# Seven-product pieces whose weight sums are made partly by accumulating transfers, in a two-block transformer kernel

## What is computed

```python
x = x + jnp.square(jax.nn.relu(h @ w_ff1[i])) @ w_ff2[i]
...
def swiglu(x, w_gate, w_up, w_down):
    return (jax.nn.silu(x @ w_gate) * (x @ w_up)) @ w_down
```

## Time and profile before

| | |
|---|---|
| median of three runs | 1417.21 us |
| the profiled execution, its own time | 1417.31 us |
| its span | 1415.5 us |
| TensorE busy (matmul / weight load) | 1408.9 / 1200.0 us |
| VectorE, ScalarE, GpSimd busy | 1159.3, 809.4, 26.6 us |
| read from HBM | 246.59 MB, 175 GB/s |

### The profile page before, as it was taken

The page is one execution under the profiler, slowest core; times in us unless marked ns, Lnnn a source line. Parts: engine busy times, 40 slices in busy tenths (PEclk is TensorE's granted clock), DMA queues, the critical chain, the costliest instruction groups (busy, mean ns, idle before and its releaser), DMA issues.

```text
span 1415.5 us, 22899 instructions
## 1 busy us (share of the span) xinstructions
PE 1408.9 (100%) x9209; PEld 1200.0 (85%) x9209; DVE 1159.3 (82%) x1601; ACT 809.4 (57%) x1095; POOL 26.6 (2%) x93
## 2 busy tenths in 40 slices
PE   9999999999999999999999999999999999999999
PEld 8988778888888888889878888888888887888887
DVE  6876776898877998988868888888888798688886
ACT  7735474655446655555766555556555557665552
POOL 0000000000001100000000000000000000000000
PEclk9999999999999999999999999999999999999999
DMA  8441335555555555455334554545545453355543
GB/s 336 152 150 62 105 107 207 177 181 208 194 215 179 192 195 195 176 195 197 135 120 174 186 199 181 208 174 195 196 179 202 161 177 146 115 203 188 182 179 116
DMA packets 36105, 249.12 MB, mean 176 GB/s; under 512 B 4128, under 2 KB 4256, under 8 KB 6688
## 3 DMA queue, kind: packets, MB, share of 16 engines
q1 hardware_dynamic: 35712, 247.46, 48.9%
q10 hardware_dynamic: 288, 0.19, 0.1%
HBM read 246.59 MB, written 1.05 MB: 175 GB/s over the span
## 4 chain that ended last, share of the span: by engine, by line
PE 97%; DMA 1%; ACT 1%; DVE 0%; issue 0%; SPq 0%; DVEq 0%; ACTq 0%
PE ps L2192 24%; PE ps L2107 16%; PE ps L2109 15%; PE ps L2108 15%; PE ps L2199 13%; PE ps L2182 2%; PE ps L2367 2%; PE ps L2181 1%; DMA raw<-ws 1%; PE ps L2281 1%; PE ps L2580 1%; PE ps L2560 1%; PE ps L2569 1%; PE ps L2352 0%; PE ps L2178 0%; ACT hi L2623 0%
## 5 line engine op out<-in xcount | busy, mean ns | idle before, releaser
L2991 DVE TENSOR_TENSOR lo<-raw,hi 128x2048 fp32r<-128x2048 f32 (+1 forms) x230 | 525.1, 2283 | 74.0 <-ACT hi L2623 71.3
L2623 ACT CAST hi<-raw 128x2048 fp32r<-128x2048 f32 (+1 forms) x230 | 438.8, 1909 | 195.5 <-PE ps L2109 105.9
L2192 PE MATMUL ps<-h,hi 128*128 128x512 f32 x1504 | 359.2, 390 | 0.0
L2192 PEld LDWEIGHTS ps<-h,hi 128*128 128x128 f32 x1504 | 276.4, 188 | 52.4
L2107 PE MATMUL ps<-hi,a 128*128 128x512 f32 x532 | 210.8, 396 | 0.0
L2109 PE MATMUL ps<-hi,a 128*128 128x512 f32 x532 | 207.6, 390 | 0.0
L2108 PE MATMUL ps<-lo,a 128*128 128x512 f32 x532 | 207.4, 390 | 0.0
L2199 PEld LDWEIGHTS ps<-h,lo 128*128 128x128 f32 x1504 | 192.2, 190 | 7.9
L2199 PE MATMUL ps<-h,lo 128*128 128x256 f32 x1504 | 194.4, 282 | 0.0
L2820 ACT COPY a<-ps 128x256 f32<-128x256 f32 x208 | 75.9, 372 | 152.6 <-PE ps L2192 80.4
L2107 PEld LDWEIGHTS ps<-hi,a 128*128 128x128 f32 x532 | 99.9, 188 | 22.2 <-issue 2.4
(11 more groups left out here) (385 smaller groups left out, 1782.5 us busy)
## 6 DMA issues: line engine op xcount, KB each, us to landing
raw<-ws SPq DMA_DIRECT2D x229, 1024.0 KB, 4.8
X<-xin SPq DMA_DIRECT2D x8, 256.0 KB, 5.5
raw<-ws SPq DMA_DIRECT2D x2, 512.0 KB, 6.5
out<-X SPq DMA_DIRECT2D x4, 256.0 KB, 2.1
small<-small SPq DMA_DIRECT2D x1, 992.5 KB, 12.8
const<-const SPq DMA_DIRECT2D x1, 900.0 KB, 6.6
a<-row SPq DMA_DIRECT2D x1, 512.0 KB, 6.0
const<-const SPq DMA_DIRECT2D x1, 388.0 KB, 14.2
```

What stands on the lines that cost most here:

```text
L2192: t = e.matmul(b2(s["slots"][u]), wh[:, k, 128 * u:128 * u + 128], h2[:, k, :, :], start=k == 0, stop=last)
L2623: e.copy(hi[j % NSPL][:, n], raw[j % NRAW][:, n]).then_inc(hi_ready, 1)
L2991: e.tensor_tensor(lo[j % NSPL][:, n], raw[j % NRAW][:, n], hi[j % NSPL][:, n].bitcast(F), ALU.subtract).then_inc(lo_ready, 1)
```

## The change

Gated down projections take seven products in pieces 1, 3, 4, 5, 6 and 7 of nine. For them there are two sets of `WL`, `WH`, `WS`, used in turn, so that a piece's sums wait for product 4 of the seven-product piece two before it; the second set lies where the normed activations were, free once the last up product is done. `ffn2` keeps its five pieces and its one set.

Signs are turned so that every weight sum is an addition. GpSimd issues three transfers of 256 KB for each piece: block 4 of the piece from HBM into `WS`, then, once `raw` is there, block 1 added onto block 2 inside `raw`, then, once the first has landed, block 2 from HBM added onto `WS`. ScalarE's `hi` waits for the second. VectorE's `w_sums`, now two instructions, waits for the second and the third. In the gated projections every unit but the first has the order 3, 1, 2, 7, 6, 4, 5 (the last unit 1, 2, 6, 7, 5, 4, 3), and waits for the weights' sums at its first product that uses one. `ffn2` and first units have 7, 6, 4, 5, 3, 1, 2 (the last of `ffn2` 1, 6, 7, 5, 4, 3, 2). The recombination keeps eight instructions.

```diff
@@ -28,7 +28,7 @@
-SEVENS = {"a": (1, 3, 5, 7), "s": (3, 5, 7, 9, 11)}
+SEVENS = {"a": (1, 3, 4, 5, 6, 7), "s": (3, 5, 7, 9, 11)}
...
@@ -488,14 +491,24 @@
                 self.H, self.L = acts
-                self.WL, self.WH, self.WS = (sums([128, 3, 512], R), sums([128, 3, 512], R), sums.again([128, 3, 512]))
+                self.sums = [(ar_([128, 3, 512], R), ar_([128, 3, 512], R), ar_.again([128, 3, 512])) for ar_ in sums]
                 self.ML = [mixed([128, 3, 128], R) for _ in range(n)]
...
 
-        by_src = {"a": Sevens(4, (aH, aL), Arena(14 * 4096), Arena(17 * 4096), (sgm[0], sgm[1], sgs[0])),
-                  "s": Sevens(5, (sH, sL), Arena(h_at - arena0), late_ar, (rl[0], rl[1], h_rest))}
+        by_src = {"a": Sevens(6, (aH, aL), [Arena(14 * 4096), Arena(h_at - arena0)], Arena(17 * 4096), (sgm[0], sgm[1], sgs[0])),
+                  "s": Sevens(5, (sH, sL), [Arena(h_at - arena0)], late_ar, (rl[0], rl[1], h_rest))}
+
+        def sums_before(j):
+
+            return sum(n <= j and n % NRAW == j % NRAW for n in sevens)
+
+        def sums_of(j):
+
+            src, unit = sevens[j]
+            return by_src[src].sums[unit % len(by_src[src].sums)]
+
         sevens = {}
...
@@ -596,17 +609,27 @@
 
+        summed = {}
+        high_at = {}
+
+        def sums_early(j):
+
+            if j in sevens and j not in summed:
+                src, unit = sevens[j]
+                sets = len(by_src[src].sums)
+                in_h = unit == sets - 1
+                summed[j] = [wsum_v.add() for _ in range(2)]
+                emit("w_sums", dve=1.4, j=j, nth=sum(n < j for n in sevens), own=summed[j], used=sum(n < j for n in sevens) - min(unit, sets - 1),
+                     after=freed[j - SEVENS[src][unit] - 1] if in_h else None)
+
         def split_hi():
...
             next_split["hi"] += 1
-            sums = None
+            sums_early(j)
+            emit("hi", act=1.9, j=j, after=freed.get(j - NSPL), sums=j in sevens)
             if j in sevens:
-                sums = wsum_v.n + 1
-                emit("w_sums", dve=2.6, j=j, own=[wsum_v.add() for _ in range(3)],
-                     used=sum(n < j for n in sevens), after=freed[j - NSPL] if sevens[j] == ("s", 0) else None)
-            emit("hi", act=1.9, j=j, after=freed.get(j - NSPL), sums=sums)
-            if j in sevens:
-                emit("w_hi", act=1.4, j=j, v=wsum_v.n, v_hi=wsum_a.add())
+                emit("w_hi", act=1.4, j=j, v=summed[j][-1], v_hi=wsum_a.add())
+                high_at[j] = wsum_a.n
             hi_due[j] = cur[0]
...
@@ -615,7 +638,7 @@
-                emit("w_lo", dve=1.7, j=j, v_hi=wsum_a.n, v=wsum_v.add())
+                emit("w_lo", dve=1.7, j=j, v_hi=high_at[j], v=wsum_v.add())
...
@@ -824,15 +847,21 @@
             opens, closes = unit == 0, unit == len(SEVENS[src]) - 1
-            need = {"own": unmet(needs(k + 1, 0)), "mixed": unmet((mix_v.sem, mixed[k])), "sums": unmet((wsum_v.sem, seven_at[i]))}
-            steps = (("7", extra[7]), ("6", extra[6]), ("4", main[1, 0]), ("5", extra[5]), ("3", main[0, 1]), ("1", extra[1]),
-                     ("2", main[0, 0]))
-            if closes:
-                steps = (steps[5], steps[1], steps[0], steps[3], steps[2], steps[4], steps[6])
-            for n, (which, sl) in enumerate(steps):
+            slots = {"1": extra[1], "2": main[0, 0], "3": main[0, 1], "4": main[1, 0], "5": extra[5], "6": extra[6], "7": extra[7]}
+            if src == "a" and unit:
+                order = "1267543" if closes else "3127645"
+            else:
+                order = "1675432" if closes else "7645312"
+            first_sum = min(order.index(which) for which in "674")
+            for n, which in enumerate(order):
+                need = {}
+                if n == 0:
+                    need.update(lo=(lo_ready, i + 1), own=unmet(needs(k + 1, 0)), mixed=unmet((mix_v.sem, mixed[k])))
+                if n == first_sum:
+                    need.update(sums=unmet((wsum_v.sem, seven_at[i])))
                 apart = which in "1567"
-                emit("seven", i=i, which=which, k=k, src=src, unit=unit, slot=sl, opens=apart and opens, closes=apart and closes,
-                     frees=which == "4", uses=which == "2", need=need if n == 0 else {})
+                emit("seven", i=i, which=which, k=k, src=src, unit=unit, slot=slots[which], opens=apart and opens,
+                     closes=apart and closes, frees=which == "4", uses=n == 6, need=need)
                 yield "pe"
...
@@ -2267,7 +2295,7 @@
-                    elif s["uses"]:
+                    if s["uses"]:
...
@@ -2618,13 +2646,13 @@
                     if s["sums"]:
-                        e.wait_ge(wsum_v.sem, s["sums"])
+                        e.wait_ge(sum_in[j % NRAW], 16 * sums_before(j))
                     n = slice(0 if j else PIECE // 2, PIECE)
...
                     e.wait_ge(wsum_v.sem, s["v"])
-                    z = by_src[sevens[s["j"]][0]]
-                    e.copy(z.WH[:, :, :], z.WS[:, :, :]).then_inc(wsum_a.sem, 1)
+                    _, WH, WS = sums_of(s["j"])
+                    e.copy(WH[:, :, :], WS[:, :, :]).then_inc(wsum_a.sem, 1)
                 elif kind == "seven_copy":
...
@@ -2970,11 +2998,11 @@
                     e.tensor_tensor(z[:, 1, :], a[:, 0, first], a[:, 0, second], ALU.subtract)
-                    e.tensor_tensor(a[:, 0, second], a[:, 0, second], a[:, 1, second], ALU.add).then_inc(mix_v.sem, 1)
+                    e.tensor_tensor(a[:, 0, second], a[:, 0, second], a[:, 1, second], ALU.subtract).then_inc(mix_v.sem, 1)
                     e.wait_ge(mix_v.sem, v[0])
...
                     e.wait_ge(mix_v.sem, v[1])
-                    e.tensor_tensor(z[:, 2, :], a[:, 1, first], z[:, 0, :], ALU.subtract).then_inc(mix_v.sem, 1)
+                    e.tensor_tensor(z[:, 2, :], a[:, 1, first], z[:, 0, :], ALU.add).then_inc(mix_v.sem, 1)
 
...
@@ -3001,22 +3029,16 @@
                     w = raw[s["j"] % NRAW][:, :].rearrange("p (q n) -> p q n", q=4)
-                    e.wait_ge(raw_in[s["j"] % NRAW], 16 * (s["j"] // NRAW + 1))
-                    if s["used"]:
-                        e.wait_ge(wsum_used.sem, s["used"])
-                    if s["after"]:
-                        e.wait_ge(s["after"][0], s["after"][1])
-                    WS = by_src[sevens[s["j"]][0]].WS
-                    e.tensor_tensor(WS[:, 1, :], w[:, 3, :], w[:, 1, :], ALU.subtract)
-                    e.tensor_tensor(w[:, 1, :], w[:, 1, :], w[:, 0, :], ALU.subtract).then_inc(wsum_v.sem, 1)
+                    e.wait_ge(sum_in[s["j"] % NRAW], 16 * sums_before(s["j"]))
+                    e.wait_ge(third_in[s["nth"] % 2], 16 * (s["nth"] // 2 + 1))
+                    _, _, WS = sums_of(s["j"])
+                    e.tensor_tensor(WS[:, 0, :], WS[:, 1, :], w[:, 0, :], ALU.add).then_inc(wsum_v.sem, 1)
                     e.wait_ge(wsum_v.sem, s["own"][0])
-                    e.tensor_tensor(WS[:, 0, :], w[:, 3, :], w[:, 1, :], ALU.subtract).then_inc(wsum_v.sem, 1)
-                    e.wait_ge(wsum_v.sem, s["own"][1])
-                    e.tensor_tensor(WS[:, 2, :], w[:, 2, :], WS[:, 0, :], ALU.subtract).then_inc(wsum_v.sem, 1)
+                    e.tensor_tensor(WS[:, 2, :], w[:, 2, :], WS[:, 0, :], ALU.add).then_inc(wsum_v.sem, 1)
                 elif kind == "w_lo":
                     e.wait_ge(wsum_a.sem, s["v_hi"])
-                    z = by_src[sevens[s["j"]][0]]
-                    e.tensor_tensor(z.WL[:, :, :], z.WS[:, :, :], z.WH[:, :, :].bitcast(F), ALU.subtract).then_inc(wsum_v.sem, 1)
+                    WL, WH, WS = sums_of(s["j"])
+                    e.tensor_tensor(WL[:, :, :], WS[:, :, :], WH[:, :, :].bitcast(F), ALU.subtract).then_inc(wsum_v.sem, 1)
                 elif kind == "seven_add":
...
@@ -3031,21 +3053,19 @@
                     ready(five)
-                    t = e.scalar_tensor_tensor(to[0, 1], banks[five.b][:, :], f[0], to[0, 1], ALU.mult, ALU.add)
-                    t.then_inc(seven_v.sem, 1)
+                    e.wait_ge(seven_v.sem, v[0])
+                    e.tensor_tensor(copy, banks[five.b][:, :], u, ALU.subtract).then_inc(seven_v.sem, 1)
                     ready(seven)
-                    e.wait_ge(seven_v.sem, v[0])
                     e.tensor_tensor(w, banks[seven.b][:, :], u, ALU.add).then_inc(seven_v.sem, 1)
-                    t = e.scalar_tensor_tensor(to[1, 1], banks[five.b][:, :], f[1], to[1, 1], ALU.mult, ALU.add)
-                    t.then_inc(seven_v.sem, 1)
                     e.wait_ge(seven_v.sem, v[1])
-                    t = e.scalar_tensor_tensor(to[0, 1], u, f[0], to[0, 1], ALU.mult, ALU.add)
+                    t = e.scalar_tensor_tensor(to[0, 1], copy, f[0], to[0, 1], ALU.mult, ALU.add)
                     t.then_inc(seven_v.sem, 1)
                     e.wait_ge(seven_v.sem, v[2])
```

(33 more changed lines are left out.)

## The result

The changed kernel took 1527.9 us (median of 6 runs, 1523.46 to 1538.07) against 1417.22 of the kernel before: a ratio of 1.0793 (1.0775 to 1.0811). The forecast was 1464, its range ended at 1502. The sign and the stages of the loss were right; the forecast loss of 46.9 us was less than half of the 110.7 measured.

The account below looks back on a forecast made before the run. The sum of TensorE's products was taken to bound the kernel unless one waits. Stalls of 38.4 us in four gated projections plus 13.9 in ffn2, less 5.4 saved, gave +46.9 on 1417.3: 1464, range 1433 to 1502.

Parts of the forecast that it names:

- the loop from product 4 to the next seven-product piece: Down projections before the change: product 4, next sums, next seven-product piece, with only 0.66 us to spare.
- D = 6.5: Time in us from the product behind product 4 to the third transfer's landing: two transfers in a row, 3.25 each.
- the quiet row: Profile row of 256 KB stores at the kernel's quiet end, 2.0 to 2.3 us each, used to price GpSimd's transfers.
- pin's 5.1: Profile row of another 256 KB transfer, pin, at 5.1 us; used in the rival of slow transfers.
- 12 us per us: Total's growth per us of D: two links in each of four gated projections, one in each of four ffn2 pieces.
- The skill's figure: GpSimd's transfers at about 2.0 us plus bytes over 436 GB/s: 2.6 each, D 5.2, total 1448.6.
- Piece 4: nothing: Gated projections: piece 4 waits for piece 1, is ready at 17.6 and due at 20.4, so no stall.
- Rival 3: Clock falls to 1.2 GHz for half the piece after each of twelve larger stalls: 29 us more, 1493; chance 0.12.
- VectorE's mixing at no cost: Gate and up products: extra mixing of about 1.6 us a piece fits on VectorE, cost 0.
- ffn2's formula: ffn2: 11.8 us needed against 8.16 available, 3.65 late at pieces 5, 7, 9 and 11, less 0.7: 13.9 us.
- the clock case: Forecast stalls with the clock at 1.2 GHz behind the twelve larger ones: 1493 us; chance 0.12.
- Slow transfers: Rival for GpSimd's two chained transfers: 5.1 to 6.0 us each, D 10.2 to 12, 1508 to 1530 us; chance 0.10.

Follow-up runs that it names:

- e5: Changed kernel with GpSimd making only the sum inside raw, not waiting for product 4, and VectorE the other three sums, still six pieces: 1426.0 us.
- e4: Changed kernel with SP's raw loads cut to the first quarter of each piece after the first three: 1515.12 us in one run.
- e3: Changed kernel with the two adding transfers as plain copies of the same bytes: 1523.52 us in one run.
- e1: Changed kernel with seven products only in gated pieces 1, 3, 5, 7, weight sums still by GpSimd's transfers: 1470.79 us.
- e7: Changed kernel with gated pieces 1, 3, 4, 5, 7; later pieces' two-block sum transferred into memory of its own, other sums on VectorE: 1440.65 us.
- e11: Changed kernel with gated pieces 1, 3, 5, 6, 7, GpSimd adding only inside raw, the other three sums on VectorE: 1416.05 us.
- e9: Changed kernel with gated pieces 1, 3, 4, 5, 7, GpSimd adding only inside raw, the other three sums on VectorE: 1419.01 us.
- e12: Changed kernel with the kernel before's gated pieces 1, 3, 5, 7, GpSimd adding only inside raw, the other three sums on VectorE: 1417.63 us.
- e8: Changed kernel with 26 additional matmuls ahead of the wait of ffn2's pieces 5, 7, 9 and 11: 1532.32 us.
- e2: Changed kernel with six gated pieces, all four sums on VectorE and no transfer by GpSimd: 1445.35 us.

## Why the prediction was wrong in size

- **What bounds the kernel.** Right: the loop from product 4 to the next seven-product piece is where nearly all of the loss stands, and taking the transfers off it (e5) makes 102 of 110.7 us go. Only 0.64 us before the first seven-product piece of ffn2 and 1.66 before piece 3 of the fourth projection lie outside it (that piece's first sum came 13.0 us after its first transfer, 1438.79 to 1451.83).
- **The failed step: D = 6.5**, as two landings of 3.25, taken "nearer the quiet row because at most one raw load runs beside them". Measured landings are 4.4 and 5.4 in the median, up to 7.6 and 8.5; D is 8.0 to 10.1 in ffn2 and 8.0 to 16.5 in the gated projections (617.21 to 633.70 in the first). The quiet row was a 256 KB store by SP's queue; even with three quarters of the raw traffic gone, GpSimd's took 3.5 and 4.2 (e4). Of the rows it had, pin's 5.1 was the nearest measure. By the prediction's own 12 us per us, the waits of 84.2 in place of 52.3 mean an effective D of 6.5 + 31.9 / 12 = 9.2, inside its bounds of 4.1 and 12. The formula was right and this term too small: 46.9 with 31.9 more for D and 27.4 for the clock gives 106.2, the difference of the spans. (That it closes so well is by construction, since D is taken from the waits; e4, where D was read off, is the test of the formula.)
- **The skill's figure.** The Trainium skill, DMA: Bandwidth & Descriptors, Anatomy of one DMA, gave 2.6 us a transfer and 1448.6 us in all. No adding transfer landed in under 3.2 us in any run, and no first load in under 3.3 (a plain copy inside SBUF reached 2.4 once, in e3); the measured landings decide, and the figure was further off than the forecast.
- **"Piece 4: nothing."** Failed. It was ready 2.8 us early by D = 6.5, and D was 13.4 there (933.15 to 946.55), with the DMA share at 1.03 and 0.98. So in the first three projections the gaps went to 4 and 6 instead of 5 and 7. With the raw loads cut (e4), and with plain transfers (e3), they stood at 5 and 7: traffic and adding together made piece 4 late.
- **Raw's second loop.** Missing from the prediction. It named hi's wait for the middle transfer and gave it no price; GpSimd then waited up to 8.12 us for raw with the third transfer queued behind it (e1). That GpSimd is not delayed was argued from its small busy share, where its order of waits was what mattered.
- **The clock.** Rival 3 was priced at 12 x 2.4 = 29 us and given 0.12; it happened, with 27.4 us (about 24 by the starts), over twelve gaps of 3.7 us and more. This is the second failed term: the sum had it at nothing. The mistake was to hold it a rival and not a consequence, for stalls of the forecast's own size bring it (3.62 us in e1 and 3.75 in e7 did). With it the forecast would have been 1493, within 2.3% of the result. That an idle array goes back to 1.2 GHz (the Trainium skill, TensorE: Matmul & The Clock Gate, Part 1) agrees with the granted 0.50 of the window 636 to 637.
- **What was right.** TensorE's share (94%, named 96), the release of each gap by VectorE's lo or low sums, the 24 matmuls and their 5.4 us, VectorE's mixing at no cost (no gap in gate and up; by the earlier trace rows it is 1.7 us a piece, not 1.6), and ffn2's formula: stall = D less what it has to spare, 6.7 us for D = 9.5 by it and 7.06 measured.
- **The range** ended at D = 9.5 at full clock, or the clock case at D = 6.5, but not at both. Slow transfers and a fallen clock come together, since long stalls make both: 1508 to 1530 for D = 10.2 to 12 was given 0.10 as if the clock stayed.

So 110.7 us are 84.2 of waits and 27.4 of longer matmuls, less 5.4, and 4.5 that the median of the runs lies over the profiled execution's span difference.

## What to carry to other kernels

A DMA that replaces two 0.69 us vector sums costs its landing, 3.4 to 9.0 us in the changed kernel, so it pays only where nothing in the loop waits for it: ask what it must wait for before it may start (here the last reader of its target), and count issue, landing and order of waits on the issuing engine as a link of the loop, priced by a row with the same traffic beside it. Where a forecast holds new stalls of TensorE, its sum must hold the lower clock behind them too (here it came behind every stall of 3.4 us and more, and behind some of 2). And before moving work off an engine, look whether spacing it suffices: three consecutive seven-product pieces at the end of a projection with one early, unchained transfer came out with no new wait in the profiled execution (e11).

## What was unexpected of the hardware

- An adding transfer of 256 KB from HBM landed in 5.4 us (median) where a plain one took 3.4, made about one and a half times the packets (10672 to 6960 over all three kinds) and took 0.86 us to issue instead of 0.54.
- The transfer inside SBUF was no quicker than those from HBM: 6.4 us with adding, 4.4 without. In e5, e9 and e12, where it is GpSimd's only transfer, it took 6.8 to 7.1 (medians), in e11 4.9.
- Behind each gap of 4.5 us and more, 7 to 12 matmuls ran some 0.43 us apart, about 2 us a gap, and no longer for a gap of 8 us than for one of 5. For short gaps the length does not decide: behind 2.97 us (e8) six did and behind 1.99 none; behind 1.98 us in e2 seven did at once (1402.03) or none at all (908.19), and behind 1.92 in e1 (943.28) five ran at full speed before the clock fell.
- Runs of the changed kernel spread by 1% (1523 to 1538), while those of the kernel before stayed within 0.08% over all its runs. A loop over DMA landings would carry their scatter into the time; that this is the reason was not tested.
